# Gated linear attention on one core: the value projections of most heads made for two heads at a time

## The reference, cut to what matters

```python
q, f_fwd, f_bwd, i, z = _split_cols(h @ w_in, C_SIZES)      # each 16 heads x 128 columns
f = lb + (1.0 - lb) * jax.nn.sigmoid(f_pre)                 # a decay for each direction
S = jnp.einsum('bhsk,bhsv->bhkv', k * jnp.exp(b[:, :, -1:] - b), v)   # state of the context
o = o + jnp.einsum('bhts,bhsv->bhtv', a, vc)                # attention within chunks
```

## Time and profile before

| what | value |
|---|---|
| median of 3 runs | 3727.15 us (3723.29 to 3727.91) |
| the profiled execution: its own time | 3728.81 us |
| its span | 3727.0 us |
| TensorE matmul busy | 3628.1 us, 97% |
| VectorE, ScalarE, GpSimd busy | 50%, 35%, 24% |
| granted TensorE clock over the span | 0.994 |

### The profile page before, as it was taken

The page is one execution under the profiler, slowest core; times in us unless marked ns, Lnnn a source line. Parts: engine busy times, 40 slices in busy tenths (PEclk is TensorE's granted clock), DMA queues, the critical chain, the costliest instruction groups (busy, mean ns, idle before and its releaser), DMA issues.

```text
span 3727.0 us, 54597 instructions
## 1 busy us (share of the span) xinstructions
PE 3628.1 (97%) x22714; PEld 2393.1 (64%) x22714; DVE 1863.3 (50%) x3332; ACT 1286.8 (35%) x2406; POOL 878.2 (24%) x896
## 2 busy tenths in 40 slices
PE   7999999999999999999999999999999999999998
PEld 3565655666667976676777667444455554778887
DVE  2333433133335343777777774354677752554543
ACT  3434434122222023444444441575454431010000
POOL 1000000001100002666666660122444530000000
PEclk9999999999999999999999999999999999999999
DMA  5112112110101121111110011121110111312221
GB/s 223 48 66 80 49 63 74 46 46 0 46 34 68 46 85 68 47 46 47 46 38 33 30 69 51 67 85 74 46 43 23 44 46 61 121 72 91 84 78 54
DMA packets 26245, 226.66 MB, mean 61 GB/s; under 512 B 2704, under 2 KB 6416, under 8 KB 10768
## 3 DMA queue, kind: packets, MB, share of 16 engines
q1 hardware_dynamic: 26000, 223.18, 16.0%
HBM read 221.07 MB, written 2.10 MB: 60 GB/s over the span
## 4 chain that ended last, share of the span: by engine, by line
PE 92%; DVE 4%; issue 1%; ACT 1%; POOL 1%; DMA 1%; SPq 0%; DVEq 0%; POOLq 0%; ACTq 0%
PE bank L1419 9%; PE bank L1345 7%; PE bank L1763 7%; PE bank L1429 5%; PE bank L1130 5%; PE bank L1230 4%; PE bank L1052 4%; PE bank L1790 4%; PE bank L1542 3%; PE bank L1409 3%; PE bank L1150 2%; PE bank L1681 2%; PE bank L1255 2%; PE bank L1501 2%; PE bank L1299 2%; PE bank L1286 2%
## 5 line engine op out<-in xcount | busy, mean ns | idle before, releaser
L1419 PE MATMUL bank<-hT,ring 128*128 128x256 f32 (+1 forms) x1024 | 349.8, 490 | 0.0
L1419 PEld LDWEIGHTS bank<-hT,ring 128*128 128x128 f32 x1024 | 189.6, 190 | 122.0 <-issue 108.1
L1130 PE MATMUL bank<-hT,ring 128*128 128x256 f32 (+1 forms) x512 | 184.4, 497 | 3.7 <-ACT hT L1861 3.7
L1542 PE MATMUL bank<-hT,ring 128*128 128x512 f32 x384 | 178.9, 599 | 4.7 <-ACT Y L1880 4.7
L1052 PE MATMUL bank<-hT,ring 128*128 128x256 f32 (+1 forms) x512 | 182.6, 494 | 0.0
L1429 PE MATMUL bank<-ring,hT 128*128 128x128 f32 x1536 | 182.0, 277 | 0.0
L1429 PEld LDWEIGHTS bank<-ring,hT 128*128 128x128 f32 x1536 | 176.3, 192 | 2.1
L1230 PE MATMUL bank<-hT,ring 128*128 128x256 f32 (+1 forms) x512 | 171.8, 486 | 0.0
L2120 ACT ACTIVATE arena<-arena 128x1024 f32<-128x1024 f32 x112 | 118.2, 1055 | 100.1 <-POOL arena L3398 57.7
L3493 POOL TENSOR_TENSOR hT<-hT,arena 128x512 f32<-128x512 f32 x3 | 5.1, 1724 | 558.6 <-ACT arena L1817 558.6
L1230 PEld LDWEIGHTS bank<-hT,ring 128*128 128x128 f32 x512 | 96.3, 190 | 62.8 <-issue 53.6
(11 more groups left out here) (571 smaller groups left out, 7802.6 us busy)
## 6 DMA issues: line engine op xcount, KB each, us to landing
ring<-in_w SPq DMA_DIRECT2D x59, 2048.0 KB, 8.2
ring<-in_w SPq DMA_DIRECT2D x17, 1536.0 KB, 6.8
ring<-in_w SPq DMA_DIRECT2D x20, 1280.0 KB, 5.6
ring<-in_w SPq DMA_DIRECT2D x13, 1024.0 KB, 4.8
ring<-in_w SPq DMA_DIRECT2D x8, 1408.0 KB, 6.1
ring<-in_w SPq DMA_DIRECT2D x17, 512.0 KB, 3.5
Y<-in_w SPq DMA_DIRECT2D x1, 2048.0 KB, 22.9
xT<-in_xT SPq DMA_DIRECT2D x4, 512.0 KB, 24.3
```

The costliest lines, as they stand in the source:

```text
L1130: ins = e.matmul(m[:, 0:b - a], w[:, k, sl(i)], hT[:, k, a:b], start=k == 0, stop=k == 7)
L1419: ins = e.matmul(m[:, 0:b - a], w[:, k, sl(1 + d)], hT[:, k, a:b], start=k == 0, stop=k == 7)
L1542: ins = e.matmul(m, w[:, k, sl(i)], hT[:, k, 0:LAT], start=k == 0, stop=k == 7)
```

## The change

It takes the value columns out of the slab of a head and makes slabs of their own: for heads 0 and 15 one each of 128 columns (`glv1`, 1024 of the slot's columns), for heads 1 and 2, 3 and 4, up to 13 and 14 one for two heads (`glv`, 2048 columns, 1024 KB). The index m counts them: m = 0 is head 0, m = 1 to 7 the pairs, m = 8 head 15. A matmul of a pair has 256 moving columns. A tile's 8 matmuls are cut in two halves (c = 0, 1), and a pair's 12 half tiles are shared out: six to the projections of the head before the pair, six to those of the pair's first head (`gl_values`). So `gl_project(0)` has all of head 0 and the first half of heads 1 and 2; `gl_project(1)` to `gl_project(13)` have six half tiles of a pair each; `gl_project(14)` and `gl_project(15)` have six half tiles of 128 columns each, for head 15. The values of odd m lie in the arena as before, those of even m in the tails of the ring's slots, which the smaller slabs leave free. The slabs `oc` that follow are larger, so their loads wait for the outputs of the heads whose values lie there.

```diff
-"zc1": 1024, "gla": 4096, "oc": 4096,
+"zc1": 1024, "gla": 3072, "glv": 2048, "glv1": 1024, "oc": 4096,
...
-["gla"] * 16 + ["oc"] * 4
+["gla"] * 16 + ["glv1"] + ["glv"] * 7 + ["glv1"] + ["oc"] * 4
...
-    for i in range(6):
-        made.append((late.pop(0) if late else []) + [("gl_v", j, i)])
+    for step in gl_values(j):
+        made.append((late.pop(0) if late else []) + step)
+    return made
+
+GL_VHEADS = [(0,)] + [(j, j + 1) for j in range(1, 14, 2)] + [(15,)]
+
+def gl_vgroups(m):
+    return [(0, 1), (2,), (3,), (4, 5)] if len(GL_VHEADS[m]) == 2 else [(0, 1, 2), (3, 4, 5)]
+
+def gl_values(j):
+    m, second = j // 2 + 1, j % 2
+    made = [[("gl_v", m, i, c)] for i in range(6) for c in range(2)]
+    made = made[6:] if second else made[:6]
+    if j == 0:
+        return [[("gl_v", 0, i, c) for c in range(2)] + half for i, half in enumerate(made)]
     return made
...
+GL_LAST = slot_of(STREAM.index("oc") + 2)
...
+        def gl_values_of(m):
+            if m % 2:
+                return gl_v_.rearrange("p (h t) -> p h t", h=2)
+            places = ring.rearrange("p (h t) -> p h t", h=NRING)[:, :, 3072:3072 + ALL]
+            first, second = [i for i in range(NRING) if i != GL_LAST]
+            return places[:, first:second + 1:second - first] if m < 8 else places[:, GL_LAST:GL_LAST + 1]
...
                 if k == 7:
                     ins.then_inc(up("gl_f_mm", (j, d, s)), 1)
+                    if d and s:
+                        give("gla", "gl_f_mm", (j, d, s))
...
-            def gl_v(j, i):
-                g = i // 4
-                if i in (0, 4):
-                    take(proj, ("gl_v", j, g), ("gl_v_copied", (j, g)))
-                w, m, (a, b) = open_w["gla"][0], bank[spot["gl_v", j, g]], TILE[i]
-                for k in range(8):
-                    ins = e.matmul(m[:, sl(i % 4)], hT[:, k, a:b], w[:, k, sl(3)], start=k == 0, stop=k == 7)
+            def gl_v(m, i, c):
+                name = OPENS["gl_v"](m, 0, 0)[0]
+                g, tiles = next((n, tiles) for n, tiles in enumerate(gl_vgroups(m)) if i in tiles)
+                if i == c == 0:
+                    slab(name, 8)
+                if c == 0 and i == tiles[0]:
+                    take(proj, ("gl_v", m, g), ("gl_v_copied", (m, g)))
+                w, (a, b) = open_w[name][0], TILE[i]
+                n = w.shape[2]
+                o = n * tiles.index(i)
+                for k in range(4 * c, 4 * c + 4):
+                    ins = e.matmul(bank[spot["gl_v", m, g]][:, o:o + n], hT[:, k, a:b], w[:, k, :], start=k == 0, stop=k == 7)
+                if c and i == tiles[-1]:
+                    ins.then_inc(up("gl_v_mm", (m, g)), 1)
+                if c and i == 5:
+                    give(name, "gl_v_mm", (m, g))
...
-                if j >= 2:
-                    q.wait_ge(*on("gl_o_mm", j - 2))
-                e.activation(gl_v_[j % 2][:, 512 * g:512 * g + n], bank[spot["gl_v", j, g]][:, 0:n],
-                             ACT.Copy).then_inc(up("gl_v_copied", (j, g)), 1)
+                n, h, a = len(tiles), len(GL_VHEADS[m]), 128 * tiles[0]
+                q.wait_ge(*on("gl_v_mm", (m, g)))
+                if m >= 2:
+                    q.wait_ge(*on("gl_o_mm", min(2 * m - 4, 12)))
...
+                o = gl_values_of(m)[:, :, a:a + 128 * n].rearrange("p h (i t) -> p h i t", t=128)
+                e.activation(o, bank[spot["gl_v", m, g]][:, 0:256 * n].rearrange("p (i h t) -> p h i t", h=2, t=128),
+                             ACT.Copy).then_inc(up("gl_v_copied", (m, g)), 1)
...
                     if i >= HEAD:
                         q.wait_ge(*on(*spot["slab", held_by(i)]))
+                    if STREAM[i] == "oc":
+                        q.wait_ge(*on("gl_o_mm", 15 if s == GL_LAST else 12))
```

More of the change, by code:

```diff
@@ L46 @@
 SIZE = {"ada0": 4096, "ada1": 4096, "zab": 1024, "zab2": 2048, "na": 3072, "gate": 1024, "mqk": 4096, "mvo": 4096,
-        "oab": 4096, "zc": 4096, "zc3": 3072, "zc1": 1024, "gla": 4096, "oc": 4096, "rg": 2560, "dz": 2048, "ba": 1024, "dn": 3072,
+        "oab": 4096, "zc": 4096, "zc3": 3072, "zc1": 1024, "gla": 3072, "glv": 2048, "glv1": 1024, "oc": 4096, "rg": 2560, "dz": 2048, "ba": 1024, "dn": 3072,
         "mixr": 2560, "mixd": 2048, "mixg": 2048, "mixp": 2048, "wo": 4096, "gu": 4096, "down": 2816}
 CUT = (["ada0"] * 6 + ["zab"] * 14 + ["zab2"] + ["na"] * 8 + ["gate"] + ["mqk", "mvo"] * 4 + ["oab"] * 4
-       + ["ada1"] * 6 + ["zc"] * 3 + ["zc3", "zc1"] + ["gla"] * 16 + ["oc"] * 4 + ["rg"] * 12 + ["ba"] + ["dz"] * 4 + ["dn"] * 8
+       + ["ada1"] * 6 + ["zc"] * 3 + ["zc3", "zc1"] + ["gla"] * 16 + ["glv1"] + ["glv"] * 7 + ["glv1"] + ["oc"] * 4 + ["rg"] * 12 + ["ba"] + ["dz"] * 4 + ["dn"] * 8
        + ["mixr"] * 8 + ["mixd"] * 2 + ["mixg", "mixp"] * 3 + ["wo"] * 2 + ["gu"] * 11 + ["down"] * 8)
@@ L470 @@
     "oab": lambda p: ["oab"] * (p > 0), "oab_": lambda s, n: ["oab"] * (s == 1 and n == 0), "zc": lambda j: ["zc"] * (j == 0), "zcp": lambda p: ["zc3" if p == 6 else "zc"] * (p % 2 == 0), "zc_": lambda c: ["zc1"] * (c == 0),
-    "gl_q": lambda j, c: ["gla"] * (c == 0), "oc7": lambda p: ["oc"], "oc_": lambda j, c: ["oc"] * (j == c == 0),
+    "gl_q": lambda j, c: ["gla"] * (c == 0), "gl_v": lambda m, i, c: ["glv" if len(GL_VHEADS[m]) == 2 else "glv1"] * (i == c == 0), "oc7": lambda p: ["oc"], "oc_": lambda j, c: ["oc"] * (j == c == 0),
     "rg_u": lambda j: ["rg"], "dz": lambda j, c: ["dz"] * (j % 2 == c == 0), "dn_gate": lambda: ["ba"],
@@ L797, in build @@
         lbm = place(64)
-        gl_q_, gl_k_, gl_b_, gl_v_ = [], [], [], []
+        gl_q_, gl_k_, gl_b_ = [], [], []
         for _ in range(2):
@@ L802, in build @@
             gl_b_.append([place(ALL), place(ALL)])
-            gl_v_.append(place(ALL))
+        gl_v_ = place(2 * ALL)
         gl_ec = place(ALL)
@@ L807, in build, with gl_v_of @@
         gl_S, gl_sq = cells(2, 1024), place(512)
+        def gl_values_of(m):
[4 more added lines that the diff above has]
+            return places[:, first:second + 1:second - first] if m < 8 else places[:, GL_LAST:GL_LAST + 1]
+        def gl_v_of(j):
+            return gl_values_of((j + 1) // 2)[:, (j + 1) % 2 if 0 < j < 15 else 0, :]
         at[0], spare[0] = 0, 10240
@@ L1447, in gl_u @@
             def gl_u(j, d):
-                v = gl_v_[j % 2]
+                v = gl_v_of(j)
                 m = take(work, ("gl_u", j, d), ("gl_state", (j, d, 3)))
                 q.wait_ge(*on("gl_kt_b", (j, d)))
-                q.wait_ge(*on("gl_v_copied", (j, 1)))
+                q.wait_ge(*on("gl_v_copied", ((j + 1) // 2, len(gl_vgroups((j + 1) // 2)) - 1)))
                 for n, c in enumerate([0, 1, 2] if d == 0 else [3, 2, 1]):
@@ L1479, in gl_o @@
                 for c in range(NT):
-                    e.matmul(m[:, sl(c)], gl_v_[j % 2][:, sl(c)], gl_AT[:, sl(c)], start=True, stop=False)
+                    e.matmul(m[:, sl(c)], gl_v_of(j)[:, sl(c)], gl_AT[:, sl(c)], start=True, stop=False)
                     for d in range(2):
@@ L2079, in gl_lg, with gl_v @@
                 e.activation(gl_ec, gl_ec, ACT.Ln).then_inc(up("gl_f_log", (j, d)), 1)
-            def gl_v(j, i):
-                if i not in (3, 5):
+            def gl_v(m, i, c):
+                g, tiles = next((n, tiles) for n, tiles in enumerate(gl_vgroups(m)) if i in tiles)
+                if c == 0 or i != tiles[-1]:
                     return
-                g, n = i // 4, 512 if i == 3 else 256
-                q.wait_ge(*on("gl_v_mm", (j, g)))
-                if j >= 2:
-                    q.wait_ge(*on("gl_o_mm", j - 2))
-                e.activation(gl_v_[j % 2][:, 512 * g:512 * g + n], bank[spot["gl_v", j, g]][:, 0:n],
-                             ACT.Copy).then_inc(up("gl_v_copied", (j, g)), 1)
+                n, h, a = len(tiles), len(GL_VHEADS[m]), 128 * tiles[0]
+                q.wait_ge(*on("gl_v_mm", (m, g)))
+                if m >= 2:
+                    q.wait_ge(*on("gl_o_mm", min(2 * m - 4, 12)))
+                if h == 1:
+                    e.activation(gl_values_of(m)[:, 0, a:a + 128 * n], bank[spot["gl_v", m, g]][:, 0:128 * n],
+                                 ACT.Copy).then_inc(up("gl_v_copied", (m, g)), 1)
+                    return
+                o = gl_values_of(m)[:, :, a:a + 128 * n].rearrange("p h (i t) -> p h i t", t=128)
+                e.activation(o, bank[spot["gl_v", m, g]][:, 0:256 * n].rearrange("p (i h t) -> p h i t", h=2, t=128),
+                             ACT.Copy).then_inc(up("gl_v_copied", (m, g)), 1)
             def gl_k(j, d):
@@ L3673, in layout @@
     W += [slab(wc, (8192 + 128 * a, 8192 + 128 * b)) for a, b in ((0, 4), (4, 8), (8, 12), (12, 15), (15, 16))]
-    W += [slab(wc, *[(2048 * a + 128 * j, 2048 * a + 128 * j + 128) for a in range(4)]) for j in range(16)]
+    W += [slab(wc, *[(2048 * a + 128 * j, 2048 * a + 128 * j + 128) for a in range(3)]) for j in range(16)]
```

(1 more changed line is left out.)

## The result

| what | before | after |
|---|---|---|
| median of 22 runs each, taken side by side | 3727.72 us | 3732.92 us |
| range of these runs | 3723.29 to 3732.72 | 3728.78 to 3739.75 |
| ratio | | 1.0015, 95% interval 1.0009 to 1.0021 |
| profiled execution, span | 3728.81, 3727.0 | 3730.77, 3729.0 |

The changed kernel is 5.2 us slower by the medians (3.4 to 7.8 us by the interval): a real slowdown, but smaller than the 7.5 us from which the forecast counted a difference. The forecast of 3729.0 in 3720 to 3736, with no change as the likeliest outcome, held; the middle value was 3.9 us low.

The account below looks back on a forecast made before the run. TensorE's matmuls were taken as the bound while other engines keep ahead. +10.35 - 4.84 - 3.58 = +1.9 us on the median of 3727.15 gave 3729.1, likeliest 3729, range 3720 to 3736, read as no change.

Parts of the forecast that it names:

- Prices: Value matmuls: 0.2156 us per merged instruction, against 0.2234 for two narrow ones; 0.062 us saved per group, 5.2 in all.
- (a): Head 0's projections: six half tiles of the pair (1, 2) added, all on the path, no added waits: +10.35 us.
- (b): Projections 1 to 13: 78 groups saving 0.062 us each, -4.84 us.
- (c): Projections 14 and 15, beside heads 13 and 14: 10.72 us less matmul work, partly turned into waits: -3.58 us.
- I take their times as fixed: Heads 13 and 14: VectorE's and GpSimd's product times at levels 3 to 6 stay unchanged, plus 0.1 us handover.
- (d): Everything else (ScalarE copies, HBM bytes, SyncE's queue, slab loads): nothing; first `oc` slab hidden with 8.5 us to spare.
- Case 1: Heads 13 and 14: the makers speed up with TensorE, all 10.72 us gained: -5.2 us, 3722; chance 0.12.
- the late `oc` slab: Head 15 waits 6.2 us for the first `oc` slab: +8.1 us, 3735; chance 0.09 with similar waits.
- the faster case: Narrow value matmuls bound by their loads; 672 fewer instructions bring 10 us or more: 3717; chance 0.04.
- case 2: Nothing gained in heads 13 and 14 or merge saves nothing: +5.5 or +6.8 us, 3733 to 3734; chance 0.1.

Follow-up runs that it names:

- e6: Kernel before, with one or two small matmuls of 384 columns ahead of level matmuls 1, 3, 4, 5, 6 of head 15: 3723.59 us, ratio 0.9992.
- e10: Changed kernel with small matmuls before levels 4, 5, 6 of heads 13 and 14 and levels 1, 3, 4, 5, 6 of head 15: 3727.23 us.
- e1: Changed kernel with every 256-column value matmul of a pair made as two of 128 columns again: 3737.04 us, ratio 1.0030.
- e2: Changed kernel, GpSimd's first key product of heads 14 and 15 waiting for VectorE's level 6 product of the head before: 3727.07 us, ratio 1.0004.
- e7: Kernel before with value matmuls of heads 14 and 15 summing only 4 of 8 model blocks, so a different result is computed: 3725.60 us.
- e9: Changed kernel run again unedited, as control and for a second trace: 3732.69 us, ratio 1.0017.
- e5: Changed kernel with e2's wait and small matmuls before levels of head 15 and levels 4, 5, 6 of heads 13 and 14: 3726.67 us.
- e3: Changed kernel with head 15's six thin value groups placed right behind q, ahead of the f groups, in both last projections: 3726.90 us.
- e4: Changed kernel with one or two small matmuls of 384 columns ahead of level matmuls 1, 3, 4, 5, 6 of head 15: 3731.12 us.
- e8: Changed kernel with e3's thin groups behind q and e4's small matmuls in head 15: 3727.56 us, ratio 1.0002.

## Why the prediction was right, and where it was not

By its own steps, from the stages of e6 (842.33) and e10 (845.98) in which the clock did not fall, the change costs 3.65 us. The forecast's sum was 1.9.

- *Prices*: right. 0.2158 us for a merged instruction against 0.2156, and 5.0 us for the whole merge (e1) against 5.2. The 81 ns of the Trainium skill ("TensorE: Matmul & The Clock Gate", "Back-to-back issue gap") for a narrow load and matmul pair would have made it 16.8 by the prediction's estimate; the row of loads and the spacing denied that before the run. The sum that the prediction gives for that case has a slip: with 16.8 saved in place of 5.2 it is 1.9 + 5.2 - 16.8 = -9.7, about 10 us faster than before, not 12.
- *(a)* +10.35 forecast, +10.36 measured, no gap.
- *(b)* -4.84 forecast, -4.56 measured. A group took 1.73 us where it had taken 1.78 to 1.79.
- *(c)* was mis-sized: -3.58 forecast, -2.09 measured. The waits before levels 4 and 5 were 1.00 and 1.11 us (1.03 and 1.25 forecast). The step that failed is "I take their times as fixed". VectorE's order was fixed, its level 6 product was not: the earlier key product met it on GpSimd, and 0.66 us became 1.41. That is 2 x 0.71 of the 1.49 us missing (e2). That these waits need nothing but thin groups is shown by e7.
- *(d)* held. SyncE issued both next slabs at 2199.04, near the 2200.1 of the forecast, and the output matmuls (2218.82) waited for none of them.
- *A term was missing*: the clock. The forecast costed a wait at its own length. But behind the waits of 2.0 us the granted clock went to 1.2 GHz in some executions, 1.7 us for each of heads 13 and 14. The first profile of the changed kernel shows none of the two, the second (e9) both. It is the likely reason that the medians differ by 5.2 to 7.0 us while work and waits differ by 3.65: over all executions the changed kernel's mean granted clock is lower by 0.0006 to 0.0009, an estimated 2.4 to 3.5 us. That filling the idle time keeps the clock up is supported by e10 against e9, in the profiles and in the mean clock of 11 executions each, and by e5; that the falls of the unprofiled executions lie in heads 13 and 14 is not shown, since only profiles show the place.
- *Rivals*: none came true as a mechanism. Case 1 is refuted by e7, the late `oc` slab by (d), and the faster case by e1. The measured 3732.92 is as near to case 2 (3733 to 3734) as to anything, but both of its conditions are refuted: the merge saved 5.0 us (e1), and 2.09 us were gained in heads 13 to 15. It came there by 3.65 us of work and waits and by the clock, which no case had. That the measured time lies well inside the range is in part luck, since the range was wide enough for a term that was not in the sum.

The fall in head 15 exists in both kernels and is no part of the difference, except by chance in a single profile.

No version of the change beats the kernel before. The best are e2, e3 and e5, level with it. The kernel before with e4's matmuls (e6) is the fastest run here, 3.2 us below it by the medians, with an interval that just reaches no difference. Between kernels with small matmuls in their waits the order is the same: e5 lies 3.1 us above e6 by the medians, 2.1 by the stage. Not tried: moving head 15's columns of the gate into heads 13 and 14 as fillers for their waits.

## What to carry to other kernels

Where one engine is the bound and others keep up by 1 to 3 us, work taken away from beside them is mostly not gained (here 2.1 of 10.7 us): cost it against the time at which each of their products is ready, not by its own length. Grouping work for two consumers moves it earlier: it is paid in full where nothing else runs, and leaves a hole at the end. And when a step starts earlier, look for what it now runs beside on engines that slow each other.

## What the runs showed that was not expected

- The two-input product of VectorE (128 x 512) took 0.66 us alone and 1.41 us beside a GpSimd product, which itself, begun in the scan ahead, took 1.38 instead of 1.00.
- The granted clock fell behind waits of 2.0 us (two shorter ones of 1.0 and 1.1 us lay ahead) in both heads in the profiles of e4 and e9, in the second of them in e1 and e7, and not in the first profile of the changed kernel, whose waits were the same. One fall cost 1.4 to 1.7 us. It never fell behind a wait that held small matmuls (the profiles of e4, e5, e6, e8 and e10); nor did it fall behind head 15's unfilled waits in e3.
- At 128 columns the weight loads ran without a pause, and still doubling the columns saved only 7.6 ns for each pair of instructions (0.1117 to 0.2158 / 2 = 0.1079 us for 128 columns).
